# Value pages as 64 gathers of two pages each, issued by GpSimd, and one ScalarE copy moved in its queue

## What is computed

```python
def decoder_layer(x, c, attend, s0, ...):
    mod = silu(c) @ w_ada + b_ada                       # six modulation vectors
    h = rms_norm(x, norm1_g) * (1 + scale1) + shift1
    q_a, k_a, v_a, q_g, k_g, v_g, og_g, gk_lr, gate_a, gate_b = split(h @ w_in)
    o_a = attend(rms_norm(q_a), rms_norm(k_a), v_a)     # block-sparse attention, top 3 blocks and the own one
    o_g, s_new = gla_chunked(q_g, k_g, v_g, log_sigmoid(gk_lr @ w_gk2 + b_gk) / 16, s0)
    o_g = rms_norm(o_g, o_norm_g) * silu(og_g)
    x = x + gate1 * ((sigmoid(gate_a) * (o_a @ w_branch_a) + sigmoid(gate_b) * (o_g @ w_branch_b)) @ w_out)
    return x + gate2 * hier_moe(...), k_a, v_a, s_new   # 32 experts

def one(qb, kn, vn, pages):                             # attention of one sample sequence
    k_past = cache_k[layer, pages].reshape(2048, 8, 64) # 16 pages of 128 tokens
    v_past = cache_v[layer, pages].reshape(2048, 8, 64)
    return moba_sequence(qb, concat(k_past, kn), concat(v_past, vn), rel_bias, 2048)
```

## Time and profile before

| | us |
|---|---|
| median of 3 runs | 1284.29 |
| lowest and highest | 1284.11, 1284.72 |
| the profiled execution's own time | 1289.69 |
| its span in the profile | 1288.0 |
| PE busy in the span | 1165.9 (91%) |
| DVE busy | 542.8 (42%) |
| ACT busy | 226.8 (18%) |
| POOL busy | 220.4 (17%) |

### The profile page before, as it was taken

The page is one execution under the profiler, slowest core; times in us unless marked ns, Lnnn a source line. Parts: engine busy times, 40 slices in busy tenths (PEclk is TensorE's granted clock), DMA queues, the critical chain, the costliest instruction groups (busy, mean ns, idle before and its releaser), DMA issues.

```text
span 1288.0 us, 20469 instructions
## 1 busy us (share of the span) xinstructions
PE 1165.9 (91%) x7817; PEld 734.0 (57%) x7817; DVE 542.8 (42%) x1138; ACT 226.8 (18%) x511; POOL 220.4 (17%) x275
## 2 busy tenths in 40 slices
PE   4899998899999999999999998999988788787897
PEld 2344443465667668888887456665544454444464
DVE  3398967463454554454444456222211111111112
ACT  4221225331322321101100222000000000000000
POOL 1432344200110112510000001111111111111001
PEclk9999999999999999999999996999999999989989
DMA  9997999997444443233434637999999999999994
GB/s 369 365 284 271 358 372 386 365 394 294 126 125 146 128 128 93 58 89 89 123 131 179 229 95 248 417 418 413 417 418 419 415 419 416 416 417 419 414 412 159
DMA packets 118409, 368.16 MB, mean 286 GB/s; under 512 B 12620, under 2 KB 58589, under 8 KB 98982
## 3 DMA queue, kind: packets, MB, share of 16 engines
q1 hardware_dynamic: 93424, 304.44, 60.9%
q0 software_dynamic: 21328, 55.24, 13.8%
q10 hardware_dynamic: 3558, 7.13, 1.9%
HBM read 354.61 MB, written 22.36 MB: 293 GB/s over the span
## 4 chain that ended last, share of the span: by engine, by line
PE 67%; DMA 22%; DVE 4%; SPq 3%; ACT 2%; issue 2%; POOL 0%; DVEq 0%; ACTq 0%; POOLq 0%
PE ps L1988 63%; DMA hx<-in_w_exp_up 7%; DMA ring<-in_w_exp_up 7%; DMA hx<-in_w_exp_gate 3%; PE ps L1999 3%; DMA ring<-in_w_in 2%; SPq L611 2%; DMA ring<-in_cache_v 1%; DMA work<-in_x_prompt 1%; DMA h_rows<-ring 1%; DVE work L1943 1%; SPq L606 1%; DVE work L1601 0%; DVE work L1607 0%; ACT hx L867 0%
## 5 line engine op out<-in xcount | busy, mean ns | idle before, releaser
L1988 PE MATMUL ps<-ring,work 128*64 128x256 f32 (+4 forms) x2064 | 302.0, 446 | 39.6 <-DMA ring<-in_w_exp_up 15.0
L1988 PEld LDWEIGHTS ps<-ring,work 128*64 128x64 f32 (+2 forms) x2064 | 160.4, 142 | 161.0 <-issue 89.1
L1988 PE MATMUL ps<-ring,hx 128*32 128x256 f32 (+3 forms) x1104 | 196.9, 449 | 10.6 <-ACT hx L890 4.2
L1988 PE MATMUL ps<-hx,ring 128*128 128x272 f32 x864 | 201.0, 393 | 2.9 <-ACT work L1032 1.9
L1988 PEld LDWEIGHTS ps<-hx,ring 128*128 128x128 f32 x864 | 163.5, 190 | 39.3 <-DVE work L1607 2.7
L1988 PEld LDWEIGHTS ps<-ring,hx 128*32 128x32 f32 (+1 forms) x1104 | 104.9, 143 | 88.5 <-issue 72.4
L1988 PE MATMUL ps<-work 128*32 128x256 f32 (+12 forms) x1186 | 135.4, 400 | 18.4 <-DVE work L1275 8.3
L1988 PE MATMUL ps<-hx,work 128*64 128x256 f32 (+3 forms) x816 | 124.2, 417 | 19.7 <-DMA hx<-in_w_exp_up 8.5
L1941 DVE TENSOR_TENSOR work<-work,ps 128x256 f32<-128x256 f32 x32 | 13.5, 421 | 249.8 <-ACT work L1220 249.8
L1988 PEld LDWEIGHTS ps<-hx,work 128*64 128x64 f32 (+2 forms) x816 | 76.6, 148 | 66.3 <-issue 29.7
L811 POOL DMA_INDIRECT out<-work x32 | 50.5, 1578 | 334.8 <-DVE work L1953 334.8
(11 more groups left out here) (340 smaller groups left out, 956.6 us busy)
## 6 DMA issues: line engine op xcount, KB each, us to landing
ring<-in_w_exp_gate SPq DMA_DIRECT2D x21, 2048.0 KB, 40.2
ring<-in_w_exp_down SPq DMA_DIRECT2D x42, 1024.0 KB, 39.1
ring<-in_w_exp_up SPq DMA_DIRECT2D x21, 2048.0 KB, 41.3
ring<-in_w_ada SPq DMA_DIRECT2D x12, 2048.0 KB, 17.3
hx<-in_w_exp_gate SPq DMA_DIRECT2D x11, 2048.0 KB, 40.0
hx<-in_w_exp_up SPq DMA_DIRECT2D x10, 2048.0 KB, 40.7
work<-in_w_exp_down SPq DMA_DIRECT2D x20, 1024.0 KB, 39.9
ring<-in_cache_v SPq DMA_DIRECT2D x64, 256.0 KB, 10.5
```

The lines of the kernel that those rows point to most:

```text
L1988: return pe.matmul(out, lhsT, rhs, start=start, stop=stop, **k)
```

## The change

- Value pages: 64 indirect transfers of GpSimd, four for each block, replace the 128 transfers of 256 KB that SyncE and GpSimd shared. Each moves 128 rows of 4 KB: two consecutive tokens are a row, so two pages fill all partitions, one in partitions 0 to 63, the other in 64 to 127. SyncE still waits at each value block's place in `stream`, and issues nothing there.
- A table `page_rows` says for each gather and partition which row to fetch. VectorE makes it at the start, of the page table copied over all partitions (`page_copy`, a new transfer) and of two constants in `cst`: so it waits for `small_tables_in` at 32 and `vec_in` at 80 ahead of its other work. Both tables lie in `ong`, whose gain is therefore loaded after the last value block has landed, by GpSimd, which waits for that.
- As a partition now holds two consecutive tokens, TensorE turns the softmax weights by pairs (`page_pair`, a read with step 2).
- In the linear attention `first_taken` stands ahead of ScalarE's wait for `la_min` and two activations, for all heads but the first.

```diff
+            if what == "v":
+                token_pairs = cache_v[0].rearrange("n (t u) h d -> (n t) (u h d)", u=2)
+                for c in range(4 if eng is nc.gpsimd else 0):
+                    eng.indirect_dma_start(slot(n)[:, 2 * AW * c:2 * AW * c + 2 * AW], None, token_pairs,
+                                           bass.IndirectOffsetOnAxis(ap=page_rows[:, 4 * i + c:4 * i + c + 1], axis=0),
+                                           bounds_check=64 * cache_v.shape[1] - 1, oob_is_err=False).then_inc(page_sem[SLOT_ORDER[n]], 16)
+                return
...
+            pool.dma_start(page_copy[:, :], bass.AP(tensor=page_table.tensor, offset=page_table.offset, ap=[[0, P], [1, DEC_B * PAGES]])).then_inc(s("small_tables_in"), 16)
...
-            pool.dma_start(ong[:, :], rows(o_norm_g, GDV)).then_inc(s("gains_in"), 16)
...
+            pool.wait_ge(s("page_rows"), 1)
             for i in range(KEY_BLOCKS):
                 half_pages("v", i)
+            for i in range(KEY_BLOCKS - 8, KEY_BLOCKS):
+                landed(pool, PAGED[("v", i)])
+            pool.dma_start(ong[:, :], rows(o_norm_g, GDV)).then_inc(s("gains_in"), 16)
...
+                if h == GH - 1:
+                    act.wait_ge(s("late_out"), 64)
+                if h:
+                    first_taken(QK, h)
                 act.wait_ge(s("la_min"), h + 1)
                 act_chain(act, act.activation(halves(cum), ps[:, 1:3, 0:HALF], ACT.Abs))
                 act_chain(act, act.activation(cum, cum, ACT.Exp, scale=-1.0))
-                if h == GH - 1:
-                    act.wait_ge(s("late_out"), 64)
-                first_taken(QK, h)
+                if h == 0:
+                    first_taken(QK, h)
...
-            dve.memset(xflat[:, 0:3072], 0.0)
+            dve.wait_ge(s("small_tables_in"), 32)
+            dve.wait_ge(s("vec_in"), 80)
+            row_in_page = st[:, 126:127]
+            link(dve.scalar_tensor_tensor(row_in_page, const("half_less_two"), -64.0, const("token_number")[:, 0:1], ALU.mult, ALU.add))
+            link(dve.tensor_scalar(row_in_page, row_in_page, -129.0, None, ALU.add))
+            link(dve.tensor_copy(page_numbers, page_copy))
+            for u in range(2):
...
+                link(dve.tensor_scalar(page_rows[rows, :].rearrange("p (g i c) -> p g i c", g=2, c=4), pairs[:, :, :, :, u], 64.0, row_in_page[rows, :],
+                                       ALU.mult, ALU.add))
+            dve.memset(xflat[:, 0:3072], 0.0).then_inc(s("page_rows"), 1)
             link(dve.memset(cT.rearrange("p k c -> p (k c)"), 0.0))
```

More of the change, by code:

```diff
@@ L151, in layer_kernel @@
         far_s = sb("far_s", [P, 1])
+        page_copy, page_rows = ong[:, 0:DEC_B * PAGES].bitcast(I32), ong[:, DEC_B * PAGES:DEC_B * PAGES * 3 // 2].bitcast(I32)
         ps = ctx.enter_context(nc.psum_tensor("ps", [P, 8, 512], F32))
@@ L567, in load_pages @@
             what, i = pieces
-            cache = cache_k if what == "k" else cache_v
-            for q in which:
-                pg = 8 * i + q
-                if what == "k":
-                    at = key_sequence(i) * PAGES + 8 * (i // 4 % 2) + q
-                else:
-                    at = (4 * (pg // (4 * PAGES)) + pg % 4) * PAGES + pg // 4 % PAGES
-                page = eng.value_load(ptab[0:1, at:at + 1], min_val=0, max_val=cache.shape[1] - 1)
-                src = cache[0, bass.DynSlice(page, 1)].rearrange("a t h d -> (a t) (h d)")
+            if what == "v":
[5 more added lines that the diff above has]
+                return
+            for q in which:
+                at = key_sequence(i) * PAGES + 8 * (i // 4 % 2) + q
+                page = eng.value_load(ptab[0:1, at:at + 1], min_val=0, max_val=cache_k.shape[1] - 1)
+                src = cache_k[0, bass.DynSlice(page, 1)].rearrange("a t h d -> (a t) (h d)")
                 eng.dma_start(slot(n)[:, AW * q:AW * q + AW], src).then_inc(sems[SLOT_ORDER[n]], 16)
@@ L2191, in _, with page_pair @@
             keys_folded(3)
+            def page_pair(g, page):
+                return logits[g][:, 0:PAST].rearrange("p (i t u) -> p i u t", i=PAGES // 2, u=2)[:, page // 2, page % 2, :]
             def weights_turned():
@@ L2201, in weights_turned @@
                         for page in range(4 * q, 4 * q + 4):
-                            last = turn(ps[:, (6, 1)[q % 2], P * (page % 4):P * (page % 4) + P], logits[0][:, P * page:P * page + P])
+                            last = turn(ps[:, (6, 1)[q % 2], P * (page % 4):P * (page % 4) + P], page_pair(0, page))
                     last.then_inc(s("pr_tr"), 1)
@@ L2212, in later_weights_turned @@
                     for page in range(4 * q, 4 * q + 4):
-                        last = turn(ps[:, 1, P * (page % 4):P * (page % 4) + P], logits[1][:, P * page:P * page + P])
+                        last = turn(ps[:, 1, P * (page % 4):P * (page % 4) + P], page_pair(1, page))
                 last.then_inc(s("pr_tr"), 1)
@@ L2228, in page_values @@
                     for j in range(4):
-                        q = 4 * (page % 2) + j
+                        q = 2 * j + page % 2
                         last = mm(ps[32 * j:32 * j + 32, 0, :], page_weights(g, page)[:, 32 * j:32 * j + 32], slot(n)[:, AW * q:AW * q + AW],
```

12 lines of the change are left out of this document (7 added, 5 removed).

## The result

The changed kernel takes **1293.24 us**, median of 5 runs (1291.41 to 1295.19), against 1284.29 us before: the ratio is 1.0070, 95% interval 1.0058 to 1.0081, so it is 0.7% slower. The prediction was 1282.1 us, faster than before, within 1280.0 to 1290.0: the time lies 3.2 us above that range, and the change made the kernel slower. The medians in this document leave out four executions that fell in a slower state: one of the kernel before (1307.67 us), one of the kernel with the table later (6597.62, which nothing on record explains) and two of the kernel with all pages into 64 partitions (1344.27 and 1345.15).

The account below looks back on a forecast made before the run. It took full DMA (share 1.03) to cause TensorE's 4.3 us of value waits. +4.1 - 4.3 - 0.8 + 0.7 - 1.9 = -2.2 on the profiled 1289.7, less 5.4 to the median, gave 1282.1 us; range 1280.0 to 1290.0.

Parts of the forecast that it names:

- start: Row table on VectorE before its first work: TensorE reaches the key stage later, +4.1 us, bounds 3 and 6.0.
- value waits that go: TensorE's waits for value blocks 11 (1.45 us) and 12 (2.83 us) vanish: -4.3 us.
- clock: TensorE's lower clock after the wait for value block 12 partly avoided: -0.8 us, bounds -1.5 and 0.
- new wait at block 15: TensorE waits for the last value block, fetched by GpSimd's gathers at 1.36 us each: +0.7 us, bounds 0 and 12.
- ScalarE's copy: Linear attention, heads 1 to 3: the copy moves ahead of two activations, removing three waits of 0.64 us: -1.9 us.
- the cover of 1.94 at the third projection: TensorE's existing wait for the third block of w_in absorbs 1.94 us of the 6.0 us delay from the start.
- The chain: Start: VectorE's table work, TensorE's bias product and turns, VectorE's four operations, then ScalarE's root at 23.8 us, 6.0 late.
- the issue rival: Value stage, 166 to 260 us: GpSimd's gather issue is the bound, from 1.37 us a gather; priced at 1289 us, chance 0.26.
- The rule on VectorE and GpSimd: Trainium skill: descriptors made by GpSimd stand still while VectorE runs in a mode taking their shared port pair; no size given.
- its three terms for the gathers: Value stage: vanished waits -4.3 us, TensorE's clock -0.8, wait at block 15 +0.7.
- The rival that the start costs nothing: Start: the table's delay is covered by something unseen; total 1278 us, chance 0.05.
- The one that the value waits came of buffers freed late: Value stage: late buffers, not full DMA, caused the waits, which return 4.1 us later; total 1286.5 us, chance 0.07.

Follow-up runs that it names:

- second trace of before: Kernel before, unchanged, run and profiled again: median 1284.13 us, ratio 0.9997; its traced execution took 1284.61 us, span 1282.9.
- start part alone: Kernel before plus copied page table, VectorE's waits and row table (unused), late load of ong; value pages and ScalarE's queue as before: 1291.17 us, ratio 1.0049.

## Why the prediction was wrong, point by point

The terms of the sum, and what the changed kernel's trace shows for each against the second trace of before:

| term | forecast, us | traces, us |
|---|---|---|
| start | +4.1 | +9.6 |
| value waits that go | -4.3 | -1.7 |
| clock | -0.8 | about 0 |
| new wait at block 15 | +0.7 | +3.7 |
| ScalarE's copy | -1.9 | -2.7 |
| sum | -2.2 | +8.9 |

The measured times differ by +9.0 and the two spans by +8.6. Two steps failed: the start was put too low, and the gathers were forecast as a gain and are a loss, because the waits that they take away were mostly those of one execution and because the landing of the last gather was taken too short.

**The base of the sum.** The sum was made against a trace 5.4 us above the median, and 5.4 was subtracted at the end. But two of its terms, the value waits of 4.28 us and the cover of 1.94 at the third projection, are 6.2 us that the trace nearer the median has only as 1.72 and 0. The excess was counted twice: once as a gain of the change, and once as the distance to the median. With the rows of the second trace the same steps give a value term of -1.7 and no cover. That alone moves the forecast up by 2.6 + 1.9 = 4.5 us, to 1286.6.

**Start, +4.1 forecast, 9.6 in the trace, 6.3 in the time of the start part alone.** The chain was the right one and the term mis-sized. 1.9 us of it are the cover at the third projection, which the second trace does not have. The chain came 8.6 us late at ScalarE's root (26.40 for 17.80), not 6.0: 2.0 because `vec_in` was complete at 17.27 and not 15.28, as in the kernel with the copied page table alone (17.05), and 0.7 because the clear started 0.71 us behind the last table operation. The five operations themselves took 1.21, forecast 1.1. "Nothing in the key stage takes it away" was right. Behind it, in the trace of the start part alone, 9.1 us at the third projection (53.85, 62.95) are 8.6 at block 13, 7.0 behind 270 us, where the kernel before had a clock fall, and 7.0 by the spans.

**Value waits, -4.3.** They did go, in every kernel with gathers but the one with pages into 64 partitions, but they were 1.7 us in the comparable trace, and the late start alone removed a part of them (1.18 us are left in the start part).

**Clock, -0.8.** The fall behind block 12's wait went, and a new one came behind block 15's: 2.84 and 1.54 us for what takes 1.92 and 0.87, +1.6 us. The second trace of before has a fall of its own later (a product of 2.94 us at 268.38 that took 2.10 in the changed kernel), which gives that much back. What the clock does there is about even, and the gain of 0.8 is not to be had.

**Gathers and block 15, +0.7, measured 3.70.** The undisturbed pace was 1.30 us, better than the 1.36 taken. Over all 63 distances it was 1.37 on the mean (86.5 us), because some gathers were held up: just where the issue rival was to begin, and 0.8 us more than the forecast's 85.7. The last gather started at 255.66 and not 251.7. The other 3.2 us of that are the first gather's, which started at 169.16 instead of 166, because the start was later. At 1.30 throughout the last would have started at 251.1, so 4.6 us were lost on the way. The rows show most of that:

```profile
169.16 1.96 POOL L573 DMA_INDIRECT ring<-in_cache_v,ong  x1 [2.74 <-PE ps L2009]
...
196.88 2.55 POOL L573 DMA_INDIRECT ring<-in_cache_v,ong  x1 [0.99 <-PE ps L2009]
...
210.44 1.72 POOL L573 DMA_INDIRECT ring<-in_cache_v,ong  x1 [0.30 <-issue]
```

Beside them VectorE ran:

```profile
169.69 1.30 DVE L1425 TENSOR_SCALAR work<-work,stats 128x2080 f32<-128x2080 f32 x1
...
196.53 2.02 DVE L1415 TENSOR_TENSOR work<-work,stats 128x1792 f32<-128x1792 f32 x1
...
209.99 1.30 DVE L1425 TENSOR_SCALAR work<-work,stats 128x2080 f32<-128x2080 f32 x1
```

Three gathers took 0.96, 1.55 and 0.72 us more than the usual 1.00, each beside one of VectorE's long operations on SBUF, and 0.69 us went into a wait for a buffer. The six traces of kernels whose value pages come by 64 gathers all have three such gathers beside the same operations, and the ends lie too regularly for chance. The first gather started 0.08 to 0.53 us before its operation and ended 0.12 to 0.13 us behind the operation's end in all six; the other two started 0.12 to 0.46 us after theirs and ended 0.87 to 0.88 us behind its end in all six. VectorE's operations took 1.30 and 2.02 or 2.03 us in each of them, so it is the gather that is held and not VectorE. No run moved those operations.

The rule on VectorE and GpSimd that the prediction cites from the Trainium skill fits the two gathers beside TENSOR_SCALAR, 1.7 us. This operation took 0.63 ns for an element of a partition, against 1.13 for the TENSOR_TENSOR. The third gather, 1.55 us, stood beside the TENSOR_TENSOR, of which the prediction's sentence says nothing. And not every operation holds a gather: the transposes of 128x4096 (4.43 us each, 1.08 ns an element) ran beside gathers of 1.00 us, and a TENSOR_REDUCE of 2.31 us beside one of 1.09.

The end is what decided: block 15 was there 10.3 us behind the start of the last gather (255.66 to 266.00), because SyncE's 2 MB and more for the linear attention started at 248.76 and shared DMA with the last gathers. With SyncE held back it took 7.1 us (254.38 to 261.45). The prediction named this, took 5.2 us from the quickest gather, and gave the wait a bound of 12. It was the right cause with the wrong end of the bound: 10.2, the median under the experts' stream in the earlier trace rows, was the nearer row. In the prediction's own steps, block 15 was to be there at 256.9, which is 0.7 ahead of TensorE at 257.6. The last gather started 4.0 us later than that, it landed 5.1 us later behind its start, and TensorE came 4.7 us later: -0.7 + 4.0 + 5.1 - 4.7 = 3.7, the wait in the trace.

**ScalarE's copy, -1.9.** Right in kind and too small: 2.7 in the trace and 3.2 in the time.

**The balance in time.** Start part +6.3, copy -3.2, and the changed kernel +9.0: the gathers account for the rest, +5.9, with what the parts do to each other. Without the late start they cost 0.42% (1.0017 against 0.9975), 5.4 us; their trace has +3.1 at block 15, +1.6 behind it by the clock, and a span that is 5.5 us longer. The prediction had its three terms for the gathers at -4.4. So the gathers were off by about 10 us, in size and sign, and the start by 2.2 in the time.

**The rivals.** The issue of GpSimd as the bound was priced at 1289 and was the nearest. Its point, 1.37 us a gather, was met on the mean and not passed, and its mechanism cost 0.8 us of the last gather's start. The lack of a second issuing engine shows in another way, as a DMA share of 0.96 where gathers were slow, from 180 to 210 us, and as later loads that pass the last gathers. The rival that the start costs nothing is refuted by the start part alone, +6.3. The one that the value waits came of buffers freed late is refuted by the gathers: the same products free the buffers, and no block ahead of block 15 made TensorE wait in any of the six traces with 64 gathers.

## What to carry to other kernels

Before a trace is used for a sum, ask whether its own excess over the median is made of the waits that the change is to remove; a second trace of the same kernel settles that. A table that is needed in the middle of a kernel belongs in a hole of its engine, not ahead of the first chain: moving it was worth 7 to 8 us of the 9 that the changed kernel lost. When one engine takes over all transfers of a stage, see who now loads ahead: the queue that became free sends its next loads beside the last of the stage, and a wait there was worth 2.9 to 4.4 us in two pairs of kernels. And ask what the one engine does beside the others' long operations: while it stands still, nobody else issues.

The best versions here are the changed kernel with the table and its copy late and SyncE held at block 14 (1280.10), and the one with every other block by gathers (1280.17), both 0.3% faster than the kernel before. Neither can be told from the ScalarE copy alone (1281.42), which is three lines.

## What the hardware showed that I had not expected

- An indirect gather of 128 rows of 4 KB takes GpSimd 1.00 us and the next starts 0.30 later: 403 GB/s from one engine. From 210 to 240 us DMA moved 388 to 407 GB/s in the six traces with 64 gathers, where pages of 256 KB into 128 partitions had 385 or 386 in five.
- A gather under way beside one of three long VectorE operations ended 0.12 to 0.13 or 0.87 to 0.88 us behind the end of that operation, in each of six traces.
- Pages of 64 rows of 4 KB into 64 partitions move 219 GB/s at a DMA share of 1.05, so the share does not give the loss away.
- One small transfer more at the start, 512 B into each of 128 partitions, went with tables of another queue that were complete at 16.85 to 17.38 us in each of five traces, against 15.05 to 16.19 in the nine without it: 1.8 us later on the mean.
- Two executions of the same kernel, 5.1 us apart in time, had 6.2 and 1.7 us of waits for DMA in front of the third projection and the value blocks.
